# Turning the forgetting heads' probabilities and all heads' results by VectorE's 32x32 blocks and a pass through scratch memory instead of by TensorE

## The reference

```python
s = jnp.einsum('bqhd,bkhd->bhqk', q, k) * HEAD_DIM ** -0.5 + c_q - c_k   # masked
p = jax.nn.softmax(s, axis=-1)
fo = rms_norm(jnp.einsum('bhqk,bkhd->bqhd', p, v), fox_norm_w)
...
o = rms_norm(o, gdn_norm_w) * jax.nn.silu(z)                             # a GDN head
out = jnp.concatenate([fo, go], axis=-1) @ w_out
```

## Time and profile before

| | before |
|---|---|
| median of 3 runs | 1889.86 us (1889.15 to 1890.69) |
| the profiled execution | 1889.48 us, its span 1887.9 us |
| TensorE busy | 1861.8 us (99%) |
| VectorE / ScalarE / GpSimd busy | 1076.7 (57%) / 729.3 (39%) / 268.5 us (14%) |
| one forgetting head | 30 us |
| one GDN head | 48 us |

### The profile page before, as it was taken

One profiled execution on the slowest core, in us unless ns is written; L12 is line 12 of the kernel. 1 busy time (PEld: TensorE's weight loads), 2 busy tenths in 40 slices (PEclk: granted clock), 3 DMA queues, 4 the chain that ended last, 5 costly groups with the idle time before them and its releaser, 6 DMA issues.

```text
span 1887.9 us, 31205 instructions
## 1 busy us (share of the span) xinstructions
PE 1861.8 (99%) x9409; PEld 1577.3 (84%) x9409; DVE 1076.7 (57%) x2353; ACT 729.3 (39%) x1467; POOL 268.5 (14%) x491
## 2 busy tenths in 40 slices
PE   7999999999999999999999999999999999999997
PEld 6999998888888888888888888888888888888886
DVE  6666666888888874664545454433334444444455
ACT  4444344554555433343333333333333333333330
POOL 2343433333333310001111110000000000000000
PEclk9999999999999999999999999999999999999999
DMA  7666674444444335245556645544445555467441
GB/s 209 184 162 160 164 172 124 117 112 112 116 112 117 117 114 164 91 129 165 156 152 165 173 128 164 162 130 129 129 129 146 145 164 162 122 167 212 162 134 67
DMA packets 317413, 270.77 MB, mean 143 GB/s; under 512 B 96600, under 2 KB 230624, under 8 KB 316704
## 3 DMA queue, kind: packets, MB, share of 16 engines
q1 hardware_dynamic: 306880, 250.90, 47.4%
q0 software_dynamic: 10464, 18.99, 4.0%
HBM read 249.73 MB, written 20.06 MB: 143 GB/s over the span
## 4 chain that ended last, share of the span: by engine, by line
PE 97%; DVE 1%; DMA 1%; SPq 1%; issue 0%; ACT 0%; DVEq 0%; POOL 0%; ACTq 0%; POOLq 0%
PE bank L298 70%; PE bank L2033 9%; PE bank L1769 7%; PE bank L1885 2%; PE bank L1245 1%; PE bank L1227 1%; PE bank L1239 1%; PE bank L1221 1%; SPq L230 1%; DMA x_res<-in_x_sample 0%; PE bank L1195 0%; DMA raw<-in_w_in 0%; PE bank L640 0%; PE bank L1288 0%; PE bank L417 0%
## 5 line engine op out<-in xcount | busy, mean ns | idle before, releaser
L274 DVE TENSOR_TENSOR w_lo<-raw,w_hi 128x512 fp32r<-128x512 f32 (+2 forms) x828 | 565.3, 691 | 620.4 <-ACT w_hi L269 617.2
L269 ACT ACTIVATE w_hi<-raw 128x512 fp32r<-128x512 f32 (+2 forms) x828 | 502.6, 616 | 838.2 <-PE bank L298 700.8
L298 PE MATMUL bank<-w_hi,aT_hi 128*128 128x512 f32 (+2 forms) x1776 | 695.7, 392 | 2.0 <-DVE aT_lo L432 1.6
L298 PE MATMUL bank<-w_hi,aT_lo 128*128 128x512 f32 (+2 forms) x1776 | 673.2, 379 | 0.0
L298 PE MATMUL bank<-w_lo,aT_hi 128*128 128x512 f32 (+2 forms) x1776 | 672.1, 378 | 0.0
L298 PEld LDWEIGHTS bank<-w_hi,aT_hi 128*128 128x128 f32 x1776 | 334.4, 188 | 60.3 <-issue 9.4
L298 PEld LDWEIGHTS bank<-w_hi,aT_lo 128*128 128x128 f32 x1776 | 333.7, 188 | 55.4
L298 PEld LDWEIGHTS bank<-w_lo,aT_hi 128*128 128x128 f32 x1776 | 334.7, 188 | 47.4
L298 PE MATMUL bank<-w_hi,hT_hi 128*128 128x512 f32 x288 | 112.0, 389 | 0.0
L298 PE MATMUL bank<-w_lo,hT_hi 128*128 128x512 f32 x288 | 112.0, 389 | 0.0
L298 PE MATMUL bank<-w_hi,hT_lo 128*128 128x512 f32 x288 | 112.0, 389 | 0.0
(11 more groups left out here) (366 smaller groups left out, 1986.8 us busy)
## 6 DMA issues: line engine op xcount, KB each, us to landing
raw<-in_ffn_w_gate SPq DMA_DIRECT2D x176, 256.0 KB, 2.7
raw<-in_ffn_w_up SPq DMA_DIRECT2D x176, 256.0 KB, 2.7
raw<-in_ffn_w_down SPq DMA_DIRECT2D x176, 256.0 KB, 3.3
raw<-in_w_in SPq DMA_DIRECT2D x128, 192.0 KB, 2.4
raw<-in_w_in SPq DMA_DIRECT2D x128, 128.0 KB, 2.3
raw<-in_w_in SPq DMA_DIRECT2D x256, 64.0 KB, 2.3
raw<-in_w_out SPq DMA_DIRECT2D x61, 256.0 KB, 3.2
h_blocks<-sg SPq DMA_DIRECT2D x11, 768.0 KB, 4.5
```

Of the source, the lines that this page charges most:

```text
L269: nc.scalar.activation(w_hi[:, g % RING, 0:width], raw[:, g % RAW, 0:width], ACT.Copy).then_inc(sem("w_high"), 1)
L274: nc.vector.tensor_tensor(w_lo[:, g % RING, 0:width], raw[:, g % RAW, 0:width], w_hi[:, g % RING, 0:width], ALU.subtract).then_inc(sem("w_ ...
L298: last = nc.tensor.matmul(acc[t][:, 0:width], l[:, k0 + n, t * P:(t + 1) * P], r[:, g % RING, 0:width], start=(n == 0 and j == 0), stop=(n ...
```

## The change

For the forgetting heads 0 to 6 four of the five probability tiles are no longer turned by TensorE. VectorE transposes their 32x32 blocks from `sc` into `fb` at slot 24, SP stores `fb` to scratch memory (`probs`) and loads it back into `pT` with the blocks exchanged, by four transfers. The products with the values move from slot 28 to slot 39, VectorE's work behind them from slots 29 and 32 to 42 and 45. The result of each of these heads, and of GDN heads 0 to 6, is turned in the same way (scratch `turns`): VectorE's blocks at slot 48, store and four loads by SP during the next head, and `mixF_hi`/`mixG_hi` (ScalarE) and `mixF_lo`/`mixG_lo` (VectorE) at slots 14 and 15 (GDN: 14 and 14) of the next head. Head 7 of either kind is turned by TensorE as before. SP's new instructions stand between its weight loads: at positions 2, 4, 10 and 12 for a forgetting head, and 10 and 11 for a GDN head.

```diff
+PROB_STORE_AT, PROB_LOAD_AT, PROB_AT = 2, 4, 39
+TURN_STORE_AT, TURN_LOAD_AT, TURN_MIX_AT = 10, 12, 14
...
+            def store_turned(sp, tile, ready, count):
+                sp.wait_ge(sem(ready), count)
+                sp.dma_start(turns.rearrange("(t p) f -> p t f", p=P), tile).then_inc(sem("o_stored"), 16)
+            def load_moved(sp, tile, count):
+                sp.wait_ge(sem("o_stored"), 16 * count)
+                for r in range(4):
+                    sp.dma_start(
+                        tile[SQUARE * r:SQUARE * (r + 1), :].rearrange("b (a c) -> b a c", c=SQUARE),
+                        turns.rearrange("(a b) (r c) -> b r a c", b=SQUARE, r=4)[:, r]).then_inc(sem("o_moved"), 16)
...  fox_pe
-                    for j, (t, c) in enumerate(((0, 0), (1, 0), (1, P), (2, P))):
-                        last = nc.tensor.transpose(b6[:, j * P:(j + 1) * P], sc[:, t, c:c + P], ident)
-                    last.then_inc(sem("f_pT_ps0"), 1)
                     nc.tensor.transpose(b7[:, 0:P], sc[:, 2, 0:P], ident).then_inc(sem("f_pT_ps1"), 1)
-                    yield 28 + later
-                    W("f_pT0")
+                    if turned_by_pe(h):
+                        yield 28
+                        pe.wait_ge(sem("f_pT0"), 1)
+                    else:
+                        yield PROB_AT
+                        pe.wait_ge(sem("o_moved"), 64 * (2 * h + 1))
...
-                    yield 41 + min(later, FIRST_TURN_LATER)
-                    W("f_o")
-                    for t in range(TT):
-                        last = nc.tensor.transpose(b3[:, t * P:(t + 1) * P], fo[:, t, :], ident)
...  fox_act
+                        yield TURN_MIX_AT
+                        act.wait_ge(sem("o_moved"), 128 * h)
+                        nc.scalar.activation(mixF_hi[:, bass.ds(h - 1, 1), :], fmoved.unsqueeze(1), ACT.Copy,
...  fox_dve
                     nc.vector.reciprocal(rden[:], den[:]).then_inc(sem("f_rden"), 1)
+                    if not turned_by_pe(h):
+                        fb_cols, sc_cols = (x[:].rearrange("p t c -> p (t c)") for x in (fb, sc))
+                        for to, c, n in ((0, 0, 1), (1, 2, 2), (3, 5, 1)):
+                            last = nc.vector.transpose(fb_cols[:, to * P:(to + n) * P], sc_cols[:, c * P:(c + n) * P])
+                        last.then_inc(sem("f_rden"), 1)
...
-                    yield 29 + later
-                    W("f_o_ps"), W("f_rden")
+                    yield 29 if turned_by_pe(h) else PROB_AT + 3
...
+                        yield 48
+                        nc.vector.transpose(fturn, fo[:].rearrange("p t c -> p (t c)"))\
+                            .then_inc(sem("f_o"), 1)
...  fox_sp
+                    def next_turn(n, h):
+                        if n == PROB_STORE_AT:
+                            sp.wait_ge(sem("f_rden"), 2 * (h + 1))
+                            sp.dma_start(probs, fb[:, 0:4, :].rearrange("p t c -> p (t c)")).then_inc(sem("o_stored"), 16)
+                        if n == PROB_LOAD_AT:
+                            sp.wait_ge(sem("o_stored"), 16 * (2 * h + 1))
+                            for r in range(4):
+                                sp.dma_start(
+                                    pT[SQUARE * r:SQUARE * (r + 1), :, :].rearrange("b n (a c) -> b n a c", c=SQUARE),
+                                    probs.rearrange("(a b) (n r c) -> b n r a c", b=SQUARE, n=4, r=4)[:, :, r])\
+                                    .then_inc(sem("o_moved"), 16)
+                        if n == TURN_STORE_AT:
+                            store_turned(sp, fturn.rearrange("p (t c) -> p t c", t=TT), "f_o", h + 1)
+                        if n == TURN_LOAD_AT:
+                            load_moved(sp, fmoved, 2 * h + 2)
...  gdn_pe, GDN heads 0 to 6
-                    yield LEVELS_DONE + 10
-                    W("g_o")
-                    for t in range(TT):
-                        last = nc.tensor.transpose(tl(turn_bank(h), t), go[:, t, :], ident)
...  gdn_dve
+                        if n == 1:
+                            W("g_mix_hi")
+                            V.scalar_tensor_tensor(out=mixG_lo[:, bass.ds(h, 1), :],
+                                                   in0=vn.rearrange("p t c -> p (t c)").unsqueeze(1), scalar=nwg2[:],
...
+                        yield 48
+                        V.transpose(R.rearrange("p t c -> p (t c)"), go[:].rearrange("p t c -> p (t c)"))\
...  next_state (SP, GDN heads)
+                    if n == STORE_AT - 2:
+                        store_turned(eng, R, "g_o", h + 2)
+                    if n == STORE_AT - 1:
+                        eng.wait_ge(sem("g_state"), h + 2)
+                        load_moved(eng, vn.rearrange("p t c -> p (t c)"), 2 * HEADS - 1 + h)
```

More of the change, by code:

```diff
@@ L109 @@
 WARM_IN = 20
-G_OWN = 25
+G_OWN = 26
 G_READ = 15
@@ L651, in encoder_layer, with turned_by_pe @@
             rows = nc.dram_tensor("rows", (ROWS * P,), F32, kind="Internal").ap()
+            turns = nc.dram_tensor("turns", (TOK, HD), F32, kind="Internal").ap()
+            probs = nc.dram_tensor("probs", (P, 4 * P), F32, kind="Internal").ap()
+            def turned_by_pe(h):
+                return isinstance(h, int) and h == HEADS - 1
+            def store_turned(sp, tile, ready, count):
[7 more added lines that the diff above has]
+                        turns.rearrange("(a b) (r c) -> b r a c", b=SQUARE, r=4)[:, r]).then_inc(sem("o_moved"), 16)
             def row_of(r, n=1):
@@ L860, in fox_pe @@
                     last.then_inc(sem("f_o_ps"), 1)
-                    yield 41 + min(later, FIRST_TURN_LATER)
-                    W("f_o")
-                    for t in range(TT):
-                        last = nc.tensor.transpose(b3[:, t * P:(t + 1) * P], fo[:, t, :], ident)
-                    last.then_inc(sem("f_oT_ps"), 1)
-                    yield 45 + later
-                    W("f_mix")
+                    if turned_by_pe(h):
+                        yield 41
+                        W("f_o")
+                        for t in range(TT):
+                            last = nc.tensor.transpose(b3[:, t * P:(t + 1) * P], fo[:, t, :], ident)
+                        last.then_inc(sem("f_oT_ps"), 1)
+                        yield 45
+                        W("f_mix")
                 def fox_act(act, h, first=False):
@@ L971, in fox_dve @@
                     last.then_inc(sem("f_max"), 1)
+                    if not first:
+                        yield 15
+                        dve.wait_ge(sem("f_mix_hi"), h)
+                        nc.vector.scalar_tensor_tensor(
+                            out=mixF_lo[:, bass.ds(h - 1, 1), :], in0=fmoved.unsqueeze(1), scalar=nwf[:],
+                            in1=mixF_hi[:, bass.ds(h - 1, 1), :], op0=ALU.mult, op1=ALU.subtract)\
+                            .then_inc(sem("f_mix"), 1)
                     yield 18 + later
@@ L999, in fox_dve @@
                         last = nc.vector.tensor_scalar(fo[:, t, :], fo[:, t, :], frs[:, t:t + 1], None, ALU.mult)
+                    if not turned_by_pe(h):
+                        after(last)
+                        yield 48
+                        nc.vector.transpose(fturn, fo[:].rearrange("p t c -> p (t c)"))\
+                            .then_inc(sem("f_o"), 1)
+                        assert own[0] == F_OWN
+                        return
+                    own[0] += 1
                     last.then_inc(sem("f_o"), 1)
-                    yield 41 + min(later, FIRST_TURN_LATER)
+                    yield 41
                     W("f_mix_hi")
@@ L1308, in gdn_pe @@
                     streams(2), streams(3).then_inc(sem("g_Ss_ps"), 1)
[L1309 to L1313 removed]
+                    if last_head(h):
+                        yield LEVELS_DONE + 10
+                        pe.wait_ge(sem("g_o"), h + 2)
+                        for t in range(TT):
+                            last = nc.tensor.transpose(tl(turn_bank(h), t), go[:, t, :], ident)
+                        last.then_inc(sem("g_oT_ps"), 1)
                 def gdn_act(act, h):
```

73 lines of the change are left out of this document (52 added, 21 removed).

## The result

| | before | after |
|---|---|---|
| median of 6 runs | 1889.51 us | 1897.74 us (1896.54 to 1902.00) |
| profiled execution, its span | 1889.5, 1887.9 us | 1896.54, 1895.0 us |

The changed kernel is slower: ratio 1.0046, 95% interval 1.0035 to 1.0056, that is 8.2 us. I had forecast 1888.7 us and given slower 0.25. The time lies above my range.

A forecast was written before the change was run, and what follows sets the result against it. TensorE, busy 1861.8 of 1887.9 us, was taken to bound the kernel. 1889.5 - 8.9 (turns removed) + 7.4 (waits for `pT`) + 0.7 (GDN levels) = 1888.7 us, range 1882 to 1896.

The forecast's parts named there:

- What the turns are worth: Tiles no longer turned by TensorE in forgetting and GDN heads: 5.4 + 3.5 = 8.9 us saved.
- Is `pT` back in time?: Forgetting heads, slot 39: last load lands at +9.0, so TensorE waits 1.05 us a head, 7.4 us for seven.
- case A: Own forecast: `pT` lands 0.45 to 1.6 us after TensorE's slot 39; 1884.5 to 1892.5, likeliest 1888.7 us; chance 0.45.
- Head 0 ... I count it like the others: Forgetting head 0, slot 24 work at slot 29, products at slot 39: counted with the same 1.05 us wait.
- The GDN levels: GDN heads, first level: `mixG_lo` ahead of Z just fits; 0.1 us wait in 7 heads, 0.7 us; bounds 0 and 3.5.
- rival D: GDN heads' levels pass on VectorE's delay: 1891.5 us if on top of late `pT`, up to 1894; chance 0.10.
- The results' way back: Store and loads from slot 48 to next head's slot 14: about 7.0 us needed of 7 to 8; cost 0.
- SP and traffic: SP's 2 us waits covered by the weight pieces, cost 0; forgetting heads' DMA share from 0.66 to about 0.84.

The follow-up runs named there:

- head 0 at slot 44: Changed kernel with head 0's product with the values at slot 44 instead of 39 and its results five slots later: 1897.0 us.
- GDN part alone: Only the GDN heads changed, forgetting heads as in the kernel before: 1890.6 us, ratio to before 0.9996 to 1.0015.
- fox part alone: Only the forgetting heads changed, GDN heads as in the kernel before: 1897.5 us, ratio to before 1.0028 to 1.0061.
- the three together: Changed kernel with head 0's product at slot 44, loads of `probs` one weight step earlier, and `mixG_lo` ahead of the fifth level: 1890.2 us.
- fox splits late: Changed kernel with the forgetting heads' splits of turned results behind the exponentials (ScalarE slot 14 to 19, VectorE 15 to 21), products at slot 39: 1904.1 us.
- loads one step earlier: Changed kernel with the four loads of `probs` at SP's position 3 instead of 4: 1893.0 us.
- split at level 5: Changed kernel with VectorE writing `mixG_lo` ahead of the fifth level of the GDN heads instead of the first: 1894.7 us.

## Why the prediction was wrong

- **What the turns are worth** (8.9 us): near as a sum, partly by luck: two errors offset each other. Without waits, heads 1 to 6 gained 0.9 us each, where I had 0.77; the GDN heads 0.3 each in the mean (2.1 in seven), where I had 0.5. The 0.1 us that each lacks, and the 0.5 more of head 5, are lost at slot 18.
- **"Is `pT` back in time?"**: the mechanism was right, the mis-sized term is the distance of the four issues. The first load went out at +4.63 (I had +4.85; of the two allowances that no row had given, the signal took 0.03 us and not 0.15, and the store's issue 0.59 to the next start and not 0.48). The issues of loads in 128-byte runs start 0.67 us apart (I had 0.5, bounds 0.38 and 1.05), so the last at +6.63 (+6.35). The loads landed 2.3 to 3.0 us later (2.65), and TensorE started at +9.0 to +9.6 in heads 1 to 6 (+9.05), in the mean +9.33. Without a wait it would have been there at +7.91. So by the distance between starts, as I had counted, the wait was 1.42 us a head where I had 1.05. (The list's 1.25, 7.5 / 6, counts from the modelled end of the product before it, which lies 0.17 us behind the next start.) This is case A: six times 0.37 is 2.2 us more, and the turns' better worth takes 0.7 of it back, near the 1.7 that these heads are off. The 2.15 us for such a load that the prediction works out from the Trainium skill, page "DMA: Bandwidth & Descriptors" (section "Anatomy of one DMA"), were too little; the section's figures are fitted to transfers that GpSimd issues, and SP issues these.
- **"Head 0 ... I count it like the others"**: this step failed. Between its turns and its product are 10 slots, not 15. I had seen the slots but not subtracted: 5 slots are 2.6 us on the very chain that I had counted to a tenth. That VectorE is less late there, the reason I gave for counting it like the others, brings the last load 2.0 us nearer, and its landing takes 1.6 us more. So by distance 1.4 + 2.6 - 2.0 + 1.6 = 3.6 us, and 3.7 were measured (3.53 in the list), in the place of 1.05; the lower clock behind it made it 1.4 us more. The waits of the eleven traces at slots 39 and 44 show the distance as the cause of most of it. That the landing comes from the collision with GpSimd's loads is not shown.
- **The GDN levels**: "I take a wait of 0.1 us" failed; it is rival D. From one level of one head I read a slack of 0.51 us for an instruction of 0.50. The split took 0.73 us out of VectorE's stretch, and TensorE lost time at the first two levels. Moving it gave back 3.0 us of the median and 2.7 in the trace, where I had 0.7: 2.0 us of the 3.4. The other 1.4 us are the turns' lower worth above. Since D came on top of A and not in its place, giving D 0.10 and pricing it only to 1894 was too little.
- **The results' way back, "Cost 0"**: right for after, where ScalarE waits 2.8 us a head and TensorE's list has no wait behind it; but it was near its edge, as head 0 at slot 44 showed.
- **SP and traffic**: right. The share was 0.78 (I had 0.84), and no weight was late through them.

Head 0, heads 1 to 6 and the GDN heads together are the 7.8 us between the forecast and the profiled execution. The medians of the parts agree: the GDN part alone, priced at 2.8 us of gain, gave none (1890.6), and the fox part alone, priced at 2.0 us of loss, lost about 8 (1897.5).

## What to carry to other kernels

When work is moved off the bounding engine by way of memory, write down for each iteration, the first above all, how far its start and its end are apart; one iteration with other offsets can cost more than all the others gain. Give such a way back its whole measured length (here 9.0 to 9.6 us from the tile that TensorE keeps to its product) and some more. Before an instruction is put among others on an engine that has no gap, look at all the hand-overs behind it, not at one; and move a wait only together with what stands behind it on its engine.

## What the runs showed of the hardware

- Some waits of TensorE between stretches in which it was busy were followed by 2 to 4 us at its lower clock level (granted 0.50 to 0.64 in the windows that it fills): one of 1.9 us (the three together), of 2.0 and 4.4 (fox splits late), 2.1 (loads one step earlier, ahead of head 0), 2.8 (fox part alone), 3.0 (split at level 5) and 3.5 (after). Others were not, and the windows show 1.00: one of 2.1 us (fox splits late), one of 2.8 (loads one step earlier), and those of 1.2 and 1.5 us in after. And before has such a stretch at 64 to 68 us with no wait ahead of it. So the length of the wait does not decide it alone; what else does is open. Behind the wait of 3.53 us the lower clock cost 1.4 us on top.
- A load of 64 KB in 512 runs of 128 bytes holds SP for 0.64 us and four follow each other at 0.67 us, about twice the 0.33 to 0.38 us of a weight load. In heads 1 to 6 of after they land in 2.3 to 3.0 us, in head 0 in 4.1 to 4.5; GpSimd's loads stand beside head 0's in every trace, with medians from 2.6 to 4.9 us.
- The store of 256 KB landed 2.1 us after its issue in the median (3.0 in head 0), 0.4 sooner than the like store of before.
- At slot 18 of a GDN head TensorE's product starts 0.05 us after VectorE's split of its weights ends, and the 0.10 to 0.15 us saved ahead of it are lost there again (split at level 5; 0.66 in head 5). That the first causes the second is my reading.
